# Head norm of the attention layers: token-major squares and Newton steps on VectorE, four transposes in place of a product with ones

## The chip, the cores and the metric

The kernel runs on one core of a Trainium2 chip. The metric is the device time of one execution in microseconds, the median of several runs. The engines are TensorE (PE in the rows, its weight loads PEld), VectorE (DVE), ScalarE (ACT), GpSimd (POOL) and SyncE (SP), which issues the weight loads from memory.

## The reference, cut to what matters

The program is a stack of four layers and a fifth block over 512 tokens of width 1024. Layers 0 and 3 are differential attention with 8 heads. Each head makes two softmax maps over causal keys, subtracts one from the other with a learned factor, multiplies by the values (128 wide), and normalises the 128 outputs of each token by their root mean square.

```python
for blk in range(S // BLOCK):                       # 4 blocks of 128 tokens
    s = einsum('bmqd,bmkd->bmqk', q[:, :, qs:ke], k[:, :, :ke]) + bias   # -inf above the diagonal
    a = softmax(s).reshape(B, H, 2, BLOCK, ke)
    a = a[:, :, 0] - lam_full * a[:, :, 1]
    outs.append(einsum('bhqk,bhkv->bhqv', a, v[:, :, :ke]))
o = concatenate(outs, axis=2)
o = rms_norm(o, subln) * (1.0 - lam_init)           # o * rsqrt(mean(o*o over 128) + 1e-6) * subln
return o.reshape(B, S, DA_V) @ w_out
```

All other layers are untouched.

## The kernel before, in words

Activations lie feature-major: 128 features on the partitions, 512 tokens along the row, 8 such chunks (`h`, and its high and low parts in fp32r, `gh`, `gl`, `xh`, `xl`). Every projection is three matmuls per chunk: high times high, high times low, low times high. Weights come in slabs of 1024x256 (`raw`), three of them in a ring: SyncE loads one when the unit of work that used its slot is done, GpSimd makes the high part `whi` (line 419), VectorE the low part `wlo` (line 1596). A unit is 8 chunks; its result lies in two banks of `proj` until ScalarE or VectorE has read it.

An attention layer (`da_mixer`, once for each engine) is a software pipeline written out by hand over 32 blocks, k = 4*head + block of 128 queries. Each engine has its own loop over k, with its own order, and semaphores between them. Every engine works strictly in its order. In iteration k TensorE does scores(k) into banks 0 and 1 of `mix`, then filling work, then transposes(k-2) of the attention map into bank 2, then values(k-3) into bank 3. The filling is the projection of the next pairs of heads: `da_fill` gives 14 chunks in 5 iterations, used up at k = 25. Q, K and V of a pair of heads are evacuated by ScalarE (`evac`, lines 1122 to 1126) and the first scores and values of a pair wait for that. From k = 26 the output projection is put in as far as heads are ready (`out_chunks`, in the order of `TAIL`, 1 or 2 chunks in each iteration); its last chunks of heads 6 and 7 come behind the loop.

VectorE does mask(k) (line 1828: adds the bias, takes the row maximum, both maps; line 1833 negates the maxima), coef(k-1) (reciprocals of the sums, lines 1840 and 1842), combine(k-1) (line 1851) and, in nine iterations, a `wlo`. ScalarE does second(k-1) (line 1144), exps(k) (line 1134, with an accumulator read each), an evacuation in nine iterations, and at_copy(k-2) (line 1152), which takes the transposed map out of bank 2.

The head norm before is feature-major. The outputs of a head lie in bank 3 as 128 features x 512 tokens. After values(4h+3) ScalarE squares the whole bank (`post_sq`, line 1093), TensorE multiplies it by a 128x128 matrix of ones into bank 2 (line 647, iteration 4h+7, right after the scores), which sums over the partitions and spreads the sum, ScalarE takes exp(-0.5*ln(sum/128 + eps)) (`post_rs`, lines 1101 and 1103, each behind a load of its function table), VectorE multiplies (`post_on`, line 1813), ScalarE writes the high part `xh` with the gain (line 1157) and VectorE the low part `xl` (line 1857). values(4h+4) waits until `post_on` has read bank 3, and transposes(4h+5) until the logarithm has read bank 2.

Of the kernel before, what the change touches and what calls it, by code (L numbers as in the profile page):

```python
# [18 lines left out]
F32 = mybir.dt.float32  # L19
# [5 lines left out]
P = 128  # L25
# [168 lines left out]
def build(nc, stream, xin, pin, pos, vecs, relb, onehot, eye, swap, picks, decay, out):  # L194
    with ExitStack() as ctx:
# [66 lines left out]
        post_rs = a("post_rs", [P, S])  # L262
# [101 lines left out]
        for name in ("start_pe start_act start_dve relu_done half_done h_half h_gate sg_half s1_added sq_done s2_added stats var_done "  # L364
                     "std_done norm_ready spread ln_u ln_full low_even half_x half_r r_hi p_in p_hi p_lo h_new scores masked negmax expd coef second "
                     "attn transposed at_copied av o_sq o_ms o_std o_rstd o_norm z_done "
                     "hg_prod hg_sc hg_pick hg_far_copied hg_keys hg_std hg_rstd hg_normed hg_turned kdup kcopy rot_in rot_mm rot_done decay_in "
                     "rsc rmul rav r_turned r_centred bias_in0 bias_in1 sw_bias0 sw_bias1 hi_even "
                     "hg_av sw_scores sw_masked sw_negmax sw_expd sw_attn sw_transposed "
                     "sw_v_turned sw_v_copied sw_at_copied sw_av sw_out sw_hi sw_lo pos_in trig z_ret rvar rstdd tap tap2 gelu2 stored "  # L370
                     "r_act u_act b_done hl_done z_lru mixed final_out lamsum lamexp lamprod").split():
            M(name)
# [64 lines left out]
        def _(pe):  # L437
# [148 lines left out]
            def da_mixer(d, layer):  # L586
# [30 lines left out]
                def transposes(k):  # L617
                    it = 32 * d + k
                    qb = k % 4
                    pe.wait_ge(M("attn"), it + 1)  # L620
                    if it:
                        pe.wait_ge(M("at_copied"), it)
                    if k > 4 and k % 4 == 1:
                        pe.wait_ge(M("o_std"), post_base(layer) + k // 4)
                    for kb in range(qb + 1):
                        last = nc.tensor.transpose(mix[:, 2, kb * P:(kb + 1) * P], da_a[:, k % 2, kb * P:(kb + 1) * P], ident[:, :])
                    last.then_inc(M("transposed"), 1)

# [26 lines left out]
                for k in range(32 + 4):  # L655
# [6 lines left out]
                    if k >= 26:  # L662
                        out_chunks(layer, (k - 26) * 12 // 10, (k - 25) * 12 // 10)
# [341 lines left out]
        def _(act):  # L1005
# [83 lines left out]
            def head_square(n, av_sem, av_value, buf):  # L1089
                act.wait_ge(av_sem, av_value)  # L1090
                if n:
                    act.wait_ge(M("o_ms"), n)
                A(buf[:, :], mix[:, 3, :], ACT.Square).then_inc(*own.sig(M("o_sq")))

            def head_std(n, buf):
                act.wait_ge(M("o_ms"), n + 1)
                if n:
                    act.wait_ge(M("o_norm"), n)
                mine()

                A(buf[:, :], mix[:, 2, :], ACT.Ln, scale=1.0 / P, bias=small[:, 252:253]).then_inc(*own.sig(M("o_std")))
                mine()
                A(buf[:, :], buf[:, :], ACT.Exp, scale=-0.5).then_inc(*own.sig(M("o_rstd")))

            def da_mixer(d, layer):
# [47 lines left out]

                def head_hi(hd):
                    n = post_base(layer) + hd
                    act.wait_ge(M("o_norm"), n + 1)
                    A(xh[:, hd, :], post_on[:, :], ACT.Copy, scale=small[:, 10 + d:11 + d]).then_inc(*own.sig(xh_ready if hd % 2 else M("hi_even")))
# [6 lines left out]
                for k in range(32 + 5):  # L1164
                    if layer == 0 and k == 18:
                        act.dma_start(bias_sw, bass.AP(tensor=table.tensor, offset=640 + 383, ap=[[1280, 16], [-1, P], [1, 256]])).then_inc(biased_sw, 16)
                    if 1 <= k < 33:
                        second(k - 1)
# [7 lines left out]
                    if k >= 7 and k % 4 == 3:  # L1176
                        head_hi((k - 7) // 4)
                    if 2 <= k < 34:
                        at_copy(k - 2)
                    if 3 <= k < 35 and (k - 3) % 4 == 3:  # L1180
                        n = post_base(layer) + (k - 3) // 4
                        head_square(n, M("av"), 32 * d + k - 3 + 1, post_sq)
                        head_std(n, post_rs)
# [392 lines left out]
        def _(dve):  # L1576
# [232 lines left out]
            def head_norm(n, buf, on):  # L1809

                dve.wait_ge(M("o_rstd"), n + 1)
                mine()
                V.tensor_tensor(on[:, :], mix[:, 3, :], buf[:, :], ALU.mult).then_inc(*own.sig(M("o_norm")))

            def da_mixer(d, layer):
# [38 lines left out]
                def head_lo(hd):  # L1854
                    dve.wait_ge(xh_ready if hd % 2 else M("hi_even"),
                                4 * X_GEN[f"mix{layer}"] + hd // 2 + 1 if hd % 2 else {0: 0, 3: 8}[layer] + hd // 2 + 1)
                    V.scalar_tensor_tensor(xl[:, hd, :], post_on[:, :], small[:, 10 + d:11 + d], xh[:, hd, :].bitcast(F32), ALU.mult, ALU.subtract)\
                        .then_inc(*own.sig(xl_ready if hd % 2 else None))
# [480 lines left out]
def post_base(layer):  # L2339

    return {0: 0, 3: 8}[layer]

# [104 lines left out]
```

## Time and profile before

| | |
|---|---|
| median of 3 runs | 3751.49 us (3750.78 to 3753.13) |
| the profiled execution | 3749.09 us |
| its span | 3746.4 us |
| granted TensorE clock, mean | 0.983 |
| TensorE busy | 3590.2 us (96%) |
| VectorE busy | 1831.0 us (49%) |
| ScalarE busy | 941.6 us (25%) |
| GpSimd busy | 847.4 us (23%) |

The span is the time between the first and the last instruction of the profile; the 2.7 us around it belong to the execution. Busy time of TensorE is modelled with overlapping matmuls, so 96% doesn't mean that it works at its peak. The two attention layers with their tails lie at 52 to 258 us (layer 0) and 2125 to 2331 us (layer 3).

### The profile page before, as it was taken

The numbers are of one execution on the slowest core, as the hardware profiler recorded it, in microseconds if no ns is written. First come the engines' busy times: TensorE is split into PE (matmuls) and PEld (weight loads), VectorE is DVE, ScalarE is ACT, GpSimd is POOL, SyncE is SP. The second block draws the span as 40 slices with busy tenths as digits, with TensorE's granted clock in tenths as the row PEclk, the third lists the DMA queues.
The fourth block names the chain that finished last, engine by engine and source line by source line (L and its number), as shares of the span: only waits on it lengthen the run. The fifth ranks groups of instructions, "written<-read, shape, count | busy, mean of one in ns | idle before, by whom it ended". The sixth has DMA issues, their size and how long they took to land.

```text
span 3746.4 us, 44571 instructions
## 1 busy us (share of the span) xinstructions
PE 3590.2 (96%) x18694; PEld 3031.5 (81%) x18694; DVE 1831.0 (49%) x2281; ACT 941.6 (25%) x1662; POOL 847.4 (23%) x374
## 2 busy tenths in 40 slices
PE   8989999999899999889999998999989999999998
PEld 6778888889788887578888876888878887788887
DVE  4555335546453346563335555553464436554434
ACT  3552001312220013531113265210141214221102
POOL 2113222211132223012223211322221111222221
PEclk9999999999999999999999999999999999999999
DMA  5312222211122222112222321222222222222222
GB/s 186 102 57 90 102 91 96 84 68 68 51 79 101 90 90 104 57 51 101 91 100 79 107 84 64 82 101 90 90 79 79 79 90 79 101 79 101 92 100 79
DMA packets 57279, 329.58 MB, mean 88 GB/s; under 512 B 5579, under 2 KB 12235, under 8 KB 20348
## 3 DMA queue, kind: packets, MB, share of 16 engines
q1 hardware_dynamic: 44604, 303.79, 22.7%
q10 hardware_dynamic: 12480, 22.96, 1.8%
q8 instruction: 151, 2.47, 0.3%
q14 instruction: 44, 0.36, 0.0%
HBM read 323.96 MB, written 8.80 MB: 89 GB/s over the span
## 4 chain that ended last, share of the span: by engine, by line
PE 87%; DVE 7%; ACT 4%; issue 1%; DMA 1%; POOL 0%; ACTq 0%; DVEq 0%
PE proj L441 23%; PE proj L443 22%; PE proj L442 22%; PE proj L540 2%; PE proj L541 2%; PE proj L542 2%; DVE s L1702 2%; PE proj L474 2%; PE proj L475 1%; PE proj L476 1%; DVE wlo L1596 1%; PE mix L613 1%; PE mix L707 1%; PE mix L517 1%; PE mix L639 1%
## 5 line engine op out<-in xcount | busy, mean ns | idle before, releaser
L419 POOL TENSOR_SCALAR whi<-raw 128x2048 fp32r<-128x2048 f32 x286 | 745.2, 2606 | 2616.4 <-DMA raw<-in_stream 2616.2
L441 PE MATMUL proj<-gh,whi 128*128 128x512 f32 x1968 | 785.0, 399 | 14.5 <-DVE wlo L1602 10.6
L443 PE MATMUL proj<-gh,wlo 128*128 128x512 f32 x1968 | 769.4, 391 | 0.0
L442 PE MATMUL proj<-gl,whi 128*128 128x512 f32 x1968 | 768.9, 391 | 0.0
L1596 DVE TENSOR_TENSOR wlo<-raw,whi 128x2048 fp32r<-128x2048 f32 x286 | 700.8, 2451 | 93.8 <-POOL whi L419 82.3
L441 PE MATMUL proj<-xh,whi 128*128 128x512 f32 x1760 | 694.7, 395 | 20.9 <-DVE wlo L1596 11.8
L443 PE MATMUL proj<-xh,wlo 128*128 128x512 f32 x1760 | 688.4, 391 | 0.0
L442 PE MATMUL proj<-xl,whi 128*128 128x512 f32 x1760 | 687.9, 391 | 0.0
L441 PEld LDWEIGHTS proj<-gh,whi 128*128 128x128 f32 x1968 | 371.4, 189 | 109.5 <-issue 19.3
L443 PEld LDWEIGHTS proj<-gh,wlo 128*128 128x128 f32 x1968 | 371.0, 189 | 79.4
L442 PEld LDWEIGHTS proj<-gl,whi 128*128 128x128 f32 x1968 | 371.6, 189 | 76.9 <-issue 2.2
L441 PEld LDWEIGHTS proj<-xh,whi 128*128 128x128 f32 x1760 | 332.4, 189 | 99.6 <-DVE wlo L1596 12.7
L443 PEld LDWEIGHTS proj<-xh,wlo 128*128 128x128 f32 x1760 | 332.1, 189 | 70.3
L442 PEld LDWEIGHTS proj<-xl,whi 128*128 128x128 f32 x1760 | 332.5, 189 | 69.0 <-issue 1.4
L1335 ACT ACTIVATE rl<-proj 128x1024 f32<-128x1024 f32 x64 | 65.7, 1027 | 951.3 <-PE proj L443 929.6
L1687 DVE TENSOR_TENSOR h<-h,proj 128x1024 f32<-128x1024 f32 (+1 forms) x76 | 80.0, 1052 | 351.4 <-PE proj L443 329.6
L2073 DVE SCALAR_TENSOR_TENSOR hid<-proj,rl 128x1024 f32<-128x1024 f32 x64 | 78.3, 1224 | 334.8 <-ACT rl L1335 334.7
L540 PE MATMUL proj<-xh,whi 128*128 128x256 f32 x640 | 191.1, 299 | 23.4 <-DVE wlo L1596 13.8
L541 PE MATMUL proj<-xl,whi 128*128 128x256 f32 x640 | 187.3, 293 | 0.0
L542 PE MATMUL proj<-xh,wlo 128*128 128x256 f32 x640 | 187.0, 292 | 0.0
L474 PE MATMUL proj<-whi,gh 128*128 128x256 f32 x512 | 152.1, 297 | 0.0
L540 PEld LDWEIGHTS proj<-xh,whi 128*128 128x128 f32 x640 | 129.3, 202 | 27.6 <-DVE wlo L1596 16.5
(295 smaller groups left out, 4417.7 us busy)
## 6 DMA issues: line engine op xcount, KB each, us to landing
raw<-in_stream SPq DMA_DIRECT2D x286, 1024.0 KB, 4.8
da_b<-bias_da ACTq DMA_DIRECT2D x16, 512.0 KB, 3.3
bias_da<-bias_rows ACTq DMA_DIRECT2D x8, 512.0 KB, 8.0
h<-in_x ACTq DMA_DIRECT2D x4, 512.0 KB, 8.9
bias_sw<-bias_table ACTq DMA_DIRECT2D x1, 2048.0 KB, 9.8
pf<-in_p ACTq DMA_DIRECT2D x4, 512.0 KB, 5.6
sw_b<-bias_sw ACTq DMA_DIRECT2D x4, 512.0 KB, 3.9
out_features<-fin SPq DMA_DIRECT2D x8, 256.0 KB, 2.3
```

The source lines that it names most:

```text
L419: nc.gpsimd.tensor_scalar(whi[:, n % RING], raw[:, n % RING], 1.0, 0.0, ALU.mult, ALU.add).then_inc(hi_done, 1)
L441: nc.tensor.matmul(out, wh, ah, start=first, stop=False, skip_group_check=check)
L442: nc.tensor.matmul(out, wh, al, start=False, stop=False, skip_group_check=check)
L443: return nc.tensor.matmul(out, wl, ah, start=False, stop=last, skip_group_check=check)
L474: nc.tensor.matmul(o, ah, wh, start=k == 0 and st % per == 0, stop=False, skip_group_check=True)
L540: nc.tensor.matmul(o, wh, ah, start=k == 0 and (j if own_banks else hf) == 0, stop=False, skip_group_check=True)
L541: nc.tensor.matmul(o, wh, al, start=False, stop=False, skip_group_check=True)
L542: last = nc.tensor.matmul(o, wl, ah, start=False, stop=k == 7, skip_group_check=True)
L1596: V.tensor_tensor(wlo[:, n % RING], raw[:, n % RING], whi[:, n % RING].bitcast(F32), ALU.subtract).then_inc(*own.sig(split_done))
L1687: ins = V.tensor_tensor(o, o, y, ALU.add)
L1702: V.tensor_tensor(total[:, :, cols(hf)], first if j == 1 else total[:, :, cols(hf)], value, ALU.add).then_inc(*own.sig(sem_))
L2073: V.scalar_tensor_tensor(hid[:, :, :], banks(u), 0.0, rl[:, :, :], ALU.max, ALU.mult).then_inc(*own.sig(rel["dve"]))
```

## The change

values(k) swaps its operands, so that a head's outputs lie in bank 3 token-major: 128 tokens on the partitions, and the 128 features of block b in columns 128b to 128b+127. ScalarE squares each block alone as soon as it is there, with the sum over the row in an accumulator (`small[:, 216+b]`). VectorE's `normalise` takes the four sums per partition, makes mean + eps, and the inverse root by a first guess from integer arithmetic on the bits and three Newton steps, all on 128x4 elements, and multiplies bank 3 by it into `post_o`. TensorE transposes the four blocks of `post_o` into bank 2 (`turn_back`), ScalarE copies them out with the gain (`take`) and makes the high part, VectorE the low part. The order in the loops changes with it: `normalise(h)` stands ahead of mask(4h+7) on VectorE, `turn_back(h)` behind scores(4h+8) on TensorE, and the high and low parts come one iteration later than before.

```diff
 # TensorE
-                    if k > 4 and k % 4 == 1:
-                        pe.wait_ge(M("o_std"), post_base(layer) + k // 4)
+                    if k >= 6 and qb == 2:
+                        pe.wait_ge(M("o_taken"), 8 * d + k // 4)
...
                     pe.wait_ge(M("at_copied"), it + 1)
+                    if k:
+                        pe.wait_ge(M("o_sq"), it)
                     if qb == 0 and k:
-                        pe.wait_ge(M("o_norm"), post_base(layer) + k // 4)
+                        pe.wait_ge(M("o_norm"), 8 * d + k // 4)
...
-                        last = nc.tensor.matmul(mix[:, 3, qb * P:(qb + 1) * P], da_v[:, g % 2, kb, hh * P:(hh + 1) * P],
-                                                da_at[:, k % 2, kb * P:(kb + 1) * P], start=kb == 0, stop=kb == qb)
+                        last = nc.tensor.matmul(mix[:, 3, qb * P:(qb + 1) * P], da_at[:, k % 2, kb * P:(kb + 1) * P],
+                                                da_v[:, g % 2, kb, hh * P:(hh + 1) * P], start=kb == 0, stop=kb == qb)
...
-                def mean_square(k):
-                    n = post_base(layer) + k // 4
-                    pe.wait_ge(M("o_sq"), n + 1)
-                    pe.wait_ge(M("at_copied"), 32 * d + min(k + 2, 32))
-                    nc.tensor.matmul(mix[:, 2, :], ones[:, :], post_sq[:, :], start=True, stop=True).then_inc(M("o_ms"), 1)
+                def turn_back(hd):
+                    pe.wait_ge(M("o_norm"), 8 * d + hd + 1)
+                    pe.wait_ge(M("at_copied"), 32 * d + min(4 * hd + 6, 32))
+                    for t in range(4):
+                        last = nc.tensor.transpose(mix[:, 2, t * P:(t + 1) * P], post_o[:, t, :], ident[:, :])
+                    last.then_inc(M("o_turned"), 1)
...
-                    if k >= 7 and k % 4 == 3:
-                        mean_square(k - 4)
+                    if k >= 8 and k % 4 == 0:
+                        turn_back((k - 8) // 4)
 # ScalarE
+                def square(k):
...
+                    act.wait_ge(M("av"), it + 1)
...
+                    A(post_sq[:, c], mix[:, 3, c], ACT.Square, accum_out=small[:, 216 + qb:217 + qb]).then_inc(*own.sig(M("o_sq")))
+                def take(hd):
+                    act.wait_ge(M("o_turned"), 8 * d + hd + 1)
...
+                    A(post_on[:, :], mix[:, 2, :], ACT.Copy, scale=small[:, 10 + d:11 + d]).then_inc(*own.sig(M("o_taken")))
...
+                    if 4 <= k < 36:
+                        square(k - 4)
                     if 1 <= k < 33:
                         second(k - 1)
...
-                    if k >= 7 and k % 4 == 3:
-                        head_hi((k - 7) // 4)
+                    if k >= 8 and k % 4 == 0:
+                        take((k - 8) // 4)
                     if 2 <= k < 34:
                         at_copy(k - 2)
-                    if 3 <= k < 35 and (k - 3) % 4 == 3:
...
+                    if k >= 8 and k % 4 == 0:
+                        head_hi((k - 8) // 4)
 # VectorE
+            def inverse_root(v, y, t):
                 mine()
+                V.tensor_scalar(t.bitcast(I32), v.bitcast(I32), 1, None, ALU.logical_shift_right).then_inc(*own.sig())
+                mine()
+                V.tensor_scalar(y.bitcast(I32), t.bitcast(I32), -1.0, 1597463007.0, ALU.mult, ALU.add).then_inc(*own.sig())
+                for i in range(3):
+                    mine()
+                    V.tensor_tensor(t, y, y, ALU.mult).then_inc(*own.sig())
+                    mine()
+                    V.scalar_tensor_tensor(t, t, -0.5, v, ALU.mult, ALU.mult).then_inc(*own.sig())
+                    mine()
+                    V.scalar_tensor_tensor(y, t, 1.5, y, ALU.add, ALU.mult).then_inc(*own.sig())
...
+                def normalise(hd):
+                    v, y, t = small[:, 220:224], small[:, 224:228], small[:, 228:232]
+                    dve.wait_ge(M("o_sq"), 32 * d + 4 * hd + 4)
+                    if hd or d:
+                        dve.wait_ge(M("o_turned"), 8 * d + hd)
+                    V.tensor_scalar(v, small[:, 216:220], 1.0 / P, RMS_EPS, ALU.mult, ALU.add).then_inc(*own.sig())
+                    inverse_root(v, y, t)
+                    mine()
+                    V.tensor_tensor(post_o[:, :, :], mix[:, 3, :].rearrange("p (t c) -> p t c", t=4),
+                                    y.rearrange("p (t c) -> p t c", c=1).broadcast_to([P, 4, P]), ALU.mult).then_inc(*own.sig(M("o_norm")))
...
                 for k in range(32 + 4):
+                    if k >= 7 and k % 4 == 3:
+                        if k < 33:
+                            coef(k - 1)
+                        normalise((k - 7) // 4)
                     if k < 32:
                         mask(k)
                     if 1 <= k < 33:
-                        coef(k - 1)
-                    if k >= 7 and k % 4 == 3:
-                        head_norm(post_base(layer) + (k - 7) // 4, post_rs, post_on)
-                    if 1 <= k < 33:
+                        if k < 7 or k % 4 != 3:
+                            coef(k - 1)
                         combine(k - 1)
-                    if k >= 8 and k % 4 == 0:
-                        head_lo((k - 8) // 4)
+                    if k >= 9 and k % 4 == 1:
+                        head_lo((k - 9) // 4)
```

## Rows read from the trace of the kernel before

**Rows 1.** The page's chain of work that ended last, by engine.
```profile
PE 87%; DVE 7%; ACT 4%; issue 1%; DMA 1%; POOL 0%; ACTq 0%; DVEq 0%
```

**Rows 2.** Windows: stretch, length, each engine's busy us, granted clock, DMA share, GB/s.
```profile
209.00:258.00 49.00, 39.20 (x176) 28.14 (x175) 21.73 (x53) 30.40 (x58) 3.89 (x1) 0.93 0.05 15
251.00:253.00 2.00, 2.00 (x6) 1.53 (x5) 0.00 (x0) 0.00 (x0) 0.00 (x0) 0.50 0.00 0
```

**Rows 3.** Waits of TensorE: us in total, times, longest.
```profile
PE mix L639 <- DVE post_on L1813: 9.0, 6, 2.1
```

**Rows 4.** Timeline around head 1: start, length, engine, line, operation.
```profile
111.09 1.06 PE L639 MATMUL mix<-da_at,da_v 128*128 128x128 f32 x8
...
112.19 0.60 ACT L1093 ACTIVATE post_sq<-mix 128x512 f32<-128x512 f32 x1 [0.19 <-PE mix L639]
...
113.14 1.13 PE L647 MATMUL mix<-post_sq,ones 128*128 128x512 f32 x2
...
113.25 0.69 DVE L1828 CUSTOM_DVE_ANT_0 da_s<-mix,da_b 128x512 f32<-128x512 f32 x1 [2.10 <-PE mix L613]
...
114.60 0.17 DVE L1833 TENSOR_SCALAR small<-small 128x2 f32<-128x2 f32 x1
...
117.57 0.71 ACT L1134 ACTIVATE da_s<-da_s,small 128x512 f32<-128x512 f32 x1
...
118.89 0.19 ACT L1134 ACTIVATION_READ_ACCUMULATOR da_s<-da_s,small 128x1 f32 x1
...
119.59 0.36 ACT L1152 ACTIVATE da_at<-mix 128x256 f32<-128x256 f32 x1
```

**Rows 5.** Timeline of TensorE, scores around heads 1 and 2.
```profile
118.74 0.49 PE L613 MATMUL mix<-da_k,da_q 64*128 64x128 f32 x4
...
136.61 1.13 PE L613 MATMUL mix<-da_k,da_q 64*128 64x512 f32 x4
...
144.57 0.61 PE L613 MATMUL mix<-da_k,da_q 64*128 64x128 f32 x4 [1.77 <-ACT da_k L1124]
```

**Rows 6.** Groups by line and shape, 52 to 258 us: busy, mean ns, idle before.
```profile
L626 PE MATMUL mix<-ident,da_a 128*128 128x128 f32 x80 | 13.9, 272 | 0.5 <-ACT da_at L1152 0.5
...
L1833 DVE TENSOR_SCALAR small<-small 128x2 f32<-128x2 f32 x32 | 8.3, 259 | 1.1
```

**Rows 7.** Timeline of VectorE at the start of the program.
```profile
32.84 1.17 DVE L1666 SCALAR_TENSOR_TENSOR small<-small 128x8 f32<-128x8 f32 x6
```

**Rows 8.** Timeline where GpSimd works on a weight slab.
```profile
87.06 3.01 POOL L419 TENSOR_SCALAR whi<-raw 128x2048 fp32r<-128x2048 f32 x1 [12.27 <-DMA raw<-in_stream]
...
88.68 1.13 PE L613 MATMUL mix<-da_k,da_q 64*128 64x512 f32 x4
...
137.66 1.91 POOL L419 TENSOR_SCALAR whi<-raw 128x2048 fp32r<-128x2048 f32 x1 [13.17 <-DMA raw<-in_stream]
...
139.13 0.46 DVE L1833 TENSOR_SCALAR small<-small 128x2 f32<-128x2 f32 x1
...
209.38 3.89 POOL L419 TENSOR_SCALAR whi<-raw 128x2048 fp32r<-128x2048 f32 x1 [16.39 <-DMA raw<-in_stream]
```

**Rows 9.** Timeline of the tail, TensorE and one VectorE row.
```profile
208.95 1.13 PE L613 MATMUL mix<-da_k,da_q 64*128 64x512 f32 x4
...
209.22 2.28 DVE L1596 TENSOR_TENSOR wlo<-raw,whi 128x2048 fp32r<-128x2048 f32 x1
...
217.80 0.79 PE L441 MATMUL proj<-xh,whi 128*128 128x512 f32 x1
...
229.28 1.13 PE L613 MATMUL mix<-da_k,da_q 64*128 64x512 f32 x4
...
235.00 0.46 PE L639 MATMUL mix<-da_at,da_v 128*128 128x128 f32 x2 [1.94 <-DVE post_on L1813]
...
241.98 1.05 PE L639 MATMUL mix<-da_at,da_v 128*128 128x128 f32 x8
...
250.11 0.47 PE L441 MATMUL proj<-xh,whi 128*128 128x512 f32 x1 [2.49 <-DVE xl L1857]
```

More of the change, by code:

```diff
@@ L261, in build @@
         post_sq = a("post_sq", [P, S])
-        post_rs = a("post_rs", [P, S])
+        post_o = a("post_o", [P, 4, P])
         post_on = a("post_on", [P, S])
@@ L365, in build @@
                      "std_done norm_ready spread ln_u ln_full low_even half_x half_r r_hi p_in p_hi p_lo h_new scores masked negmax expd coef second "
-                     "attn transposed at_copied av o_sq o_ms o_std o_rstd o_norm z_done "
+                     "attn transposed at_copied av o_sq o_norm o_turned o_taken lo_even z_done "
                      "hg_prod hg_sc hg_pick hg_far_copied hg_keys hg_std hg_rstd hg_normed hg_turned kdup kcopy rot_in rot_mm rot_done decay_in "
@@ L654, in da_mixer @@
                     pe.wait_ge(M("lamexp"), 1)
-                for k in range(32 + 4):
+                for k in range(32 + 5):
                     if k < 32:
                         scores(k)
-                    if k >= 7 and k % 4 == 3:
-                        mean_square(k - 4)
+                    if k >= 8 and k % 4 == 0:
+                        turn_back((k - 8) // 4)
                     for c in range(da_fill(k - 1), da_fill(k)):
                         chunk(c // 24 + 1, c % 24)
-                    if k >= 26:
+                    if 26 <= k < 36:
                         out_chunks(layer, (k - 26) * 12 // 10, (k - 25) * 12 // 10)
@@ L1087, in rms_chunks @@
                     A(out_hi[:, k, cols(hf)], tln[:, k % 4, :], ACT.Copy, scale=col(name, k)).then_inc(*own.sig(sem_))
[L1089 to L1103, printed above, removed]
             def da_mixer(d, layer):
@@ L1152, in at_copy @@
                     A(da_at[:, k % 2, 0:(qb + 1) * P], mix[:, 2, 0:(qb + 1) * P], ACT.Copy).then_inc(*own.sig(M("at_copied")))
+                def square(k):
+                    it, qb = 32 * d + k, k % 4
+                    c = slice(qb * P, (qb + 1) * P)
+                    act.wait_ge(M("av"), it + 1)
+                    if qb == 0 and k:
+                        act.wait_ge(M("o_norm"), 8 * d + k // 4)
+                    A(post_sq[:, c], mix[:, 3, c], ACT.Square, accum_out=small[:, 216 + qb:217 + qb]).then_inc(*own.sig(M("o_sq")))
+                def take(hd):
+                    act.wait_ge(M("o_turned"), 8 * d + hd + 1)
+                    if hd:
+                        n = hd - 1
+                        act.wait_ge(*((xl_ready, 4 * X_GEN[f"mix{layer}"] + n // 2 + 1) if n % 2 else (M("lo_even"), 4 * d + n // 2 + 1)))
+                    A(post_on[:, :], mix[:, 2, :], ACT.Copy, scale=small[:, 10 + d:11 + d]).then_inc(*own.sig(M("o_taken")))
                 def head_hi(hd):
-                    n = post_base(layer) + hd
-                    act.wait_ge(M("o_norm"), n + 1)
-                    A(xh[:, hd, :], post_on[:, :], ACT.Copy, scale=small[:, 10 + d:11 + d]).then_inc(*own.sig(xh_ready if hd % 2 else M("hi_even")))
+                    mine()
+                    A(xh[:, hd, :], post_on[:, :], ACT.Copy).then_inc(*own.sig(xh_ready if hd % 2 else M("hi_even")))
                 evac(0, 0)
@@ L1856, in head_lo @@
                                 4 * X_GEN[f"mix{layer}"] + hd // 2 + 1 if hd % 2 else {0: 0, 3: 8}[layer] + hd // 2 + 1)
-                    V.scalar_tensor_tensor(xl[:, hd, :], post_on[:, :], small[:, 10 + d:11 + d], xh[:, hd, :].bitcast(F32), ALU.mult, ALU.subtract)\
-                        .then_inc(*own.sig(xl_ready if hd % 2 else None))
+                    V.tensor_tensor(xl[:, hd, :], post_on[:, :], xh[:, hd, :].bitcast(F32), ALU.subtract)\
+                        .then_inc(*own.sig(xl_ready if hd % 2 else M("lo_even")))
+                def normalise(hd):
[5 more added lines that the diff above has]
+                    inverse_root(v, y, t)
+                    mine()
+                    V.tensor_tensor(post_o[:, :, :], mix[:, 3, :].rearrange("p (t c) -> p t c", t=4),
+                                    y.rearrange("p (t c) -> p t c", c=1).broadcast_to([P, 4, P]), ALU.mult).then_inc(*own.sig(M("o_norm")))
                 for j in range(3):
@@ L2336 @@
 RET_GATED = (5, 7, 10, 11)
-def post_base(layer):
-    return {0: 0, 3: 8}[layer]
 _ORDER = ["stream", "x", "p", "positions", "vectors", "rel_bias", "onehot", "eye", "swap", "picks", "decay"]
```

6 lines of the change are left out of this document (removed).

## The prediction

> **What bounds the kernel now.** I read the page first: TensorE holds 87% of the chain that ended last [rows 1]. So an edit counts only where it gives TensorE less to do or moves a moment at which TensorE waits. Then came the stretches of the attention layers by windows, the waits whose waiter is TensorE, and the timeline around one head. Each attention layer (0 and 3; layer 3 repeats layer 0's pattern) has a body, blocks 0 to 25, in which projection work fills TensorE, and a tail of 49 us from block 26 to the output projection, where TensorE is busy for 39 us and the granted clock averages 0.93 [rows 2]. The head norm makes TensorE wait 9.0 us for `post_on` over both layers [rows 3], and 2.49 us per layer for the last `xl` [rows 9]; nearly all of it is tail.
>
> Write k = 4h+b for block b of head h, and T for the end of values(4h+3), 0.07 us after scores(4h+3) begins. Around head 1, T is 112.15. ScalarE squares at once and the product with ones follows, while VectorE masks block 11 straight away, at 113.25. The exponentials of block 11 began only at 117.57, behind ScalarE's two table loads, two functions and one scaled copy, and the copy of block 9 out of bank 2 ended at 119.95, T + 7.8 [rows 4]. TensorE had finished scores(12) at 119.23 [rows 5] and went on filling: nothing waited for that copy.
>
> **The change part by part, TensorE's work.** The product with ones, 1.1 us in two passes [rows 4], goes. Four transposes come: one takes 0.27 us, and matmuls overlap by 0.1 to 0.16; 80 of them were busy for 13.9 us, 0.17 each [rows 6], so four take 0.65 us. The swapped operands of values cost nothing: 128 columns go through 128x128 weights either way. TensorE has 0.45 us less to do per head, 7 us in all, if nothing waits.
>
> **VectorE's chain.** New are 12 dependent operations on 4 elements (one scaling, two on integers, nine Newton) and one broadcast product of 512. Six dependent 8-element operations took 1.17 us [rows 7], so 0.20 us each: 2.4 us. The product reads PSUM like a mask of 512, 0.69 us [rows 4]; with 0.06 for handing over, 3.15 us. A small operation is bounded by 0.17 us, the negation of two maxima with nothing behind it [rows 4], and 0.26 us, the mean of those negations, held ones among them [rows 6]: 2.0 to 3.1 us for twelve. I take 0.20, from a chain of the same shape. The Trainium skill (VectorE: DVE Perf Modes, the section on the TRN2 errata) gives an fp32 tensor_tensor of N elements (N+151)/0.96 ns, 161 ns for 4: a fixed cost per instruction, which speaks against many small ones. By it the twelve would take 1.9 us, and each waiting head 0.5 us less than I sum; the trace's pitch, which includes the hand-over, is used.
>
> What is queued behind: `normalise` now stands ahead of mask(4h+3), which before ran at once. The mask, two reductions and a negation, takes 1.55 us [rows 4]. Then on ScalarE come its exponentials, 1.50 us, and at_copy(4h+1), 0.36 us [rows 4]. The new transposes write bank 2, so TensorE waits in turn_back for precisely that copy (`at_copied` 4h+6), with all its filling work queued behind. The old product waited for a copy one block earlier.
>
> **ScalarE.** One square of 0.60 us becomes four of 128 columns with an accumulator read. Bounds are 0.36, the copy of 256 columns without a read, and 0.6, the whole square [rows 4]; I take 0.45. Three of the four lie in ScalarE's idle time. Ln, Exp and both loads go, most of the 4.8 us between the square's end and 117.57 [rows 4]; a copy `take` of 0.6 us comes ahead of transposes(4h+6), under 3 chunks of filling in the body. ScalarE wins time, but its exponentials now wait for VectorE. The bias loads that it issues behind them are two heads ahead, and SP's weight loads follow TensorE's units: neither becomes late.
>
> **Sum of a body head.** 0.48 (square) + 0.05 + 3.15 (normalise) + 0.05 + 1.55 (mask) + 0.05 + 1.50 (exponentials) + 0.36 (copy) + 0.05 = T + 7.25, and 0.65 of transposes: filling resumes at T + 7.9. Before, it resumed at the end of the next scores, T + 7.1 at head 1 (heads 0 and 3 alike), and T + 8.5 at head 2 (head 4 alike), where scores wait for an evacuation to `da_k` [rows 5]. That evacuation stands ahead of the copy and adds 0.9 there. Hence 3 x 0.8 + 2 x 0.3 = 3.0 us.
>
> VectorE is also held while GpSimd works on a weight slab: a negation that began during GpSimd's 137.66 to 139.57 took 0.46 us and ended with it [rows 8]. Of normalise, operations would begin in such a stretch at head 0 (T = 88.75, GpSimd to 90.07), 0.65 us, and at head 2 (T = 136.68, to 139.57), 1.8 us [rows 8]. A slab subtraction on VectorE itself adds 0.3 at head 3. Body: 3.0 + 2.75 = 5.7 us per layer; 2.45 less if small operands are not held.
>
> **Sum of the tail.** Head 5 (T = 209.02): there are no 3 chunks of filling left, and VectorE subtracts a slab until 211.50, behind which coef(26) and then `normalise` come: it begins at T + 3.0 instead of T + 0.55, and GpSimd's hold (to 213.27 [rows 8]) adds 1.1. So the transposes end at T + 7.9 + 2.45 + 1.1 = 220.45, and filling resumes there, against 217.80 before [rows 9]: +2.65. The half-clock stretch that lies over this filling now also covers transposes, values and scores: +0.8. Head 6: filling went on behind values(28), which had waited until 235.00, 5.65 after T = 229.35; now it goes on at T + 7.9: +2.25, of which I take 0.65 as given back by the later wait for `da_at`, which then has passed: +1.6. Head 7: no mask lies between; from T = 243.03 to the waiting output chunk it was 7.1 us and is now 0.5 (square) + 3.15 + 0.75 (transposes) + 0.65 (`take`) + 0.7 (`xh`) + 0.8 (`xl`) = 6.55: -0.5 [rows 9]. Tail: +4.5.
>
> Per layer 10.2, two layers 20.4 us. The profiled execution took 3749.09 us (span 3746.4), so 3769.5; the median of the runs is 2.4 above it: 3772 us.
>
> **The rivals.** *The chain is hidden (faster).* Place: the wait of turn_back. At head 1 it vanishes if the copy lands by the end of scores(12), at 118.2 once the product is gone: the chain must be 1.1 us shorter than 7.25, so normalise at most 2.1 us. From there a head gains 0.45, and if the tail's waits go too, all that the old norm costs TensorE is won: 7 + 9.0 + 5.0 = 21 us, 3730 us. For it: ScalarE is rid of its table work. Against it: even before, the copy landed 0.7 us after the scores.
>
> *Half hidden (no change).* With a pitch of 0.15 us and no hold by GpSimd, 0.6 us less at each of 7 heads and 3.55 us of hold less per layer leave 2.5 us, 5 in two layers: 3757 us.
>
> *The clock.* The tail has two stretches at half the clock, 1.2 GHz, one of them behind the wait of 2.49 us [rows 2, 9]. A mean of 0.93 over 49 us is 3.4 us of full-speed work lost, 1.7 each [rows 2]. After, head 2 waits some 2 us, heads 5 and 6 3 us or more. If heads 0, 2, 3, 4 and 6 each bring on one more such stretch, that is 8.5 us per layer, 17 in all: 3789 us. The Trainium skill (TensorE: Matmul & The Clock Gate, Part 4, PE-mode transpose) says that a transpose does not count as activity of the array for its clock. By this rule the four transposes would not help to keep the clock where the product of 1.1 us did, which is this rival. The 160 transposes of before lie among matmuls at full clock, so its trace neither bears the rule out nor denies it.
>
> **How the numbers follow.** The wait moves to turn_back as summed: 0.60, own range 3760 to 3783 (small operations of 0.17 to 0.26 us, holds or none, tail terms half or one and a half). Clock: 0.12. Half hidden: 0.16. Hidden: 0.12. A measurement of this kernel tells a change over about 0.2%, 7.5 us, from none: slower 0.72, same 0.16, faster 0.12. The range from 3750 to 3790 takes in the half-hidden case and most of the clock's.
>
> **What would show it.** In the profile after: no table load in these layers' blocks; TensorE's transposes of `post_o` waiting for ScalarE's `da_at` copy, 1 to 2 us in the body and 3 us or more in blocks 28 and 32; twelve small VectorE operations 0.20 us apart, and the masks of 4h+3 at T + 3.7 instead of T + 1.1; each tail 4 to 5 us longer. I am wrong if those transposes wait for nothing, if the small operations run in less than 0.15 us each, or if ScalarE, rid of its loads, brings the copy forward anyway.

## The result and the profile after

The changed kernel takes 3777.03 us (median of 4 runs, 3776.55 to 3781.24), the kernel before 3751.14 us (4 runs, 3747.91 to 3753.13) on the same chip. The medians differ by 25.9 us, where 20.4 were forecast. The ratio, estimated from the single runs, is 1.0076 with a 95% interval of 1.0064 to 1.0088, or 0.76% slower; the quotient of the two medians is 1.0069. The profiled execution of the changed kernel took 3781.24 us with a span of 3779.4. It is the longest of the four, 4.2 us above their median, and 32 us above the profiled execution of before: sums over its trace have to be held against these 32 us, not against the 25.9.

The chain of work that ended last, from the page, against [rows 1]. TensorE's share fell by 2 points and VectorE's rose by 2.
```profile
PE 85%; DVE 9%; ACT 3%; issue 1%; DMA 1%; POOL 0%; ACTq 0%; DVEq 0%
```
The waits of TensorE in these layers (us in total, times, longest), against [rows 3]:
```profile
PE mix L649 <- ACT da_at L1139: 16.5, 10, 3.0
...
PE mix L641 <- DVE post_o L1877: 12.4, 6, 4.4
PE mix L613 <- ACT da_k L1111: 12.3, 4, 3.6
...
PE proj L441 <- DVE xl L1866: 4.5, 2, 2.3
...
PE mix L649 <- DVE post_o L1877: 1.6, 2, 0.8
...
PE mix L613 <- DVE small L1837: 1.5, 3, 0.6
```
L649 is the transposes of `post_o`, L641 values, L613 scores. The kernel before had 9.0 us for `post_on` [rows 3], and these:
```profile
PE mix L613 <- ACT da_k L1124: 5.6, 4, 1.8
PE proj L441 <- DVE xl L1857: 5.0, 2, 2.5
PE mix L647 <- ACT post_sq L1093: 4.4, 4, 1.5
PE mix L626 <- ACT da_at L1152: 0.9, 2, 0.5
PE mix L613 <- DVE small L1828: 0.6, 1, 0.6
```
So 25.5 us of waits became 48.8, and the largest is the one that the prediction named.

Now the windows over both attention layers whole, from the first copy to `da_q` to the first squares behind the layer. Columns: stretch, length, busy us of TensorE, its weight loads, VectorE, ScalarE, GpSimd, granted clock, DMA share, GB/s. Before:
```profile
38.00:256.00 218.00, 204.97 (x1159) 162.88 (x1158) 105.89 (x284) 117.16 (x253) 26.25 (x11) 0.98 0.28 97
...
2104.00:2328.00 224.00, 211.53 (x1195) 168.66 (x1194) 107.80 (x284) 118.42 (x253) 29.09 (x12) 0.98 0.22 76
```
After, and five stretches of layer 0 behind waits:
```profile
39.00:273.00 234.00, 208.50 (x1164) 168.85 (x1163) 121.24 (x379) 96.79 (x284) 28.40 (x11) 0.92 0.26 90
...
2123.00:2362.00 239.00, 215.10 (x1210) 174.26 (x1209) 123.19 (x380) 98.36 (x285) 30.25 (x12) 0.94 0.20 71
...
143.00:149.00 6.00, 2.28 (x11) 1.90 (x12) 5.07 (x14) 2.95 (x8) 0.00 (x0) 0.75 0.27 90
201.00:206.00 5.00, 4.80 (x23) 4.58 (x24) 2.21 (x9) 2.73 (x10) 0.00 (x0) 0.50 0.11 42
226.00:234.00 8.00, 6.09 (x23) 4.84 (x22) 3.49 (x14) 4.61 (x15) 0.00 (x0) 0.50 0.00 1
250.00:254.00 4.00, 4.00 (x14) 3.31 (x14) 0.75 (x1) 1.41 (x2) 0.00 (x0) 0.50 0.01 4
266.00:270.00 4.00, 3.61 (x9) 2.86 (x10) 0.25 (x1) 0.00 (x0) 0.00 (x0) 0.50 0.00 0
```
The two layers grow by 16 and 15 us. The long stretch between them, whose instructions are the same, took 1848 us before and 1850 after. Idle time of TensorE (length less busy) grew from 13.0 to 25.5 us in layer 0 and from 12.5 to 23.9 in layer 3. Its busy time should have fallen by 3.6 us per layer, the prediction's 0.45 per head of lighter work; it rose by 3.5 and 3.6. That is 7.1 and 7.2 us of busy time that no added work explains, and the clock column says where to look: 0.98 became 0.92 and 0.94. In layer 0 there are stretches at 0.50, which is 1.2 GHz, behind TensorE's waits at heads 4, 5, 6 and 7, and a mean of 0.75 at head 2 (at heads 2 and 4 the wait is for `da_k`). Behind the waits of 1.46 and 1.20 us at heads 0 and 1 the clock stayed at 1.00. Layer 3 is not the same: at its head 4 TensorE waited 2.30 us and kept 1.00.
```profile
2293.48 0.49 PE L613 MATMUL mix<-da_k,da_q 64*128 64x128 f32 x4 [2.30 <-ACT da_k L1111]
...
2294.00:2299.00 5.00, 5.00 (x43) 5.00 (x44) 1.81 (x8) 2.07 (x6) 0.00 (x0) 1.00 0.01 3
```
The length of a wait alone doesn't tell whether the clock falls. The kernel before had the same wait of 2.49 us for `xl` at the end of both layers; behind it the clock was 0.50 in layer 0 [rows 2] and 1.00 in layer 3:
```profile
2323.00:2328.00 5.00, 3.89 (x17) 3.25 (x18) 1.60 (x2) 0.18 (x1) 0.00 (x0) 1.00 0.00 0
```

The timeline of VectorE at head 4 (start, length, engine, line, operation), with a row of GpSimd among them:
```profile
192.72 0.17 DVE L1874 TENSOR_SCALAR small<-small 128x4 f32<-128x4 f32 x1 [1.74 <-ACT post_sq L1147]
192.92 0.17 DVE L1813 TENSOR_SCALAR small<-small 128x4 int32<-128x4 int32 x1
...
193.33 0.16 DVE L1818 TENSOR_TENSOR small<-small 128x4 f32<-128x4 f32 x1
...
194.91 0.16 DVE L1822 SCALAR_TENSOR_TENSOR small<-small 128x4 f32<-128x4 f32 x1
195.11 0.69 DVE L1877 TENSOR_TENSOR post_o<-mix,small 128x512 f32<-128x512 f32 x1
195.94 0.69 DVE L1837 CUSTOM_DVE_ANT_0 da_s<-mix,da_b 128x512 f32<-128x512 f32 x1
...
196.75 1.91 POOL L419 TENSOR_SCALAR whi<-raw 128x2048 fp32r<-128x2048 f32 x1 [15.29 <-DMA raw<-in_stream]
...
197.29 1.39 DVE L1842 TENSOR_SCALAR small<-small 128x2 f32<-128x2 f32 x1
```
Twelve small operations start 0.20 us apart. The negation behind the masks takes 1.39 us instead of 0.17 and ends with GpSimd's slab. At head 4 of layer 3 it took 0.78 us.

TensorE's scores of the last block of heads 4 to 7, and two waits of the tail:
```profile
168.05 0.70 PE L613 MATMUL mix<-da_k,da_q 64*128 64x512 f32 x2
192.21 0.70 PE L613 MATMUL mix<-da_k,da_q 64*128 64x512 f32 x2
218.29 0.70 PE L613 MATMUL mix<-da_k,da_q 64*128 64x512 f32 x2
225.66 0.77 PE L641 MATMUL mix<-da_v,da_at 128*128 128x128 f32 x2 [4.44 <-DVE post_o L1877]
242.62 0.70 PE L613 MATMUL mix<-da_k,da_q 64*128 64x512 f32 x2
249.82 1.09 PE L649 MATMUL mix<-ident,post_o 128*128 128x128 f32 x4 [3.02 <-ACT da_at L1139]
```

### The profile page after: what moved, and what is told of

Same layout as the page of the kernel before. It is cut to its first block, busy times and chain, and to the rows that moved or that the text cites. A ratio compares the mean times of both kernels' runs of the same rounds, so it can differ in the third digit from the quotient of the medians.

```text
span 3779.4 us, 44941 instructions
## 1 busy us (share of the span) xinstructions
PE 3601.9 (95%) x18726; PEld 3047.7 (81%) x18726; DVE 1869.0 (49%) x2473; ACT 901.2 (24%) x1726; POOL 850.4 (23%) x374
## 3 DMA queue, kind: packets, MB, share of 16 engines
q8 instruction: 152, 2.49, 0.3%
## 4 chain that ended last, share of the span: by engine, by line
PE 85%; DVE 9%; ACT 3%; issue 1%; DMA 1%; POOL 0%; ACTq 0%; DVEq 0%
PE proj L441 22%; PE proj L443 22%; PE proj L442 22%; PE proj L540 2%; PE proj L541 2%; PE proj L542 2%; DVE s L1703 2%; DVE wlo L1597 2%; PE proj L474 1%; PE proj L475 1%; PE proj L476 1%; PE mix L710 1%; PE mix L517 1%; PE mix L613 1%; PE mix L641 1%
## 5 line engine op out<-in xcount | busy, mean ns | idle before, releaser
L441 PEld LDWEIGHTS proj<-xh,whi 128*128 128x128 f32 x1760 | 334.9, 190 | 99.7 <-DVE wlo L1597 11.4
L414 POOL TENSOR_TENSOR xl<-h,xh 128x512 fp32r<-128x512 f32 (+1 forms) x80 | 99.3, 1243 | 233.1 <-ACT h L1082 233.1
## 6 DMA issues: line engine op xcount, KB each, us to landing
bias_sw<-bias_table ACTq DMA_DIRECT2D x1, 2048.0 KB, 10.3
```

Of the source, the lines that this page charges most:

```text
L414: nc.gpsimd.tensor_tensor(xl[:, k:k + n, cols(hf)], h[:, k:k + n, cols(hf)], xh[:, k:k + n, cols(hf)].bitcast(F32), ALU.subtract)\
L441: nc.tensor.matmul(out, wh, ah, start=first, stop=False, skip_group_check=check)
```

## The experiments

Theory W: the loss is TensorE's waits, made by the chain of square, normalise, mask, exponentials and copy. Rival C: much of it is the clock, because work behind the waits runs at 1.2 GHz. Rival O: the order on VectorE is all of it. Rival X: the four squares and their waits are the cost, and VectorE's small operations lie beside the path. Rival V: leaving out ScalarE's table loads is what the change is good for, so that a root on ScalarE would be slower still. Each run's ratio is to the kernel before on the same chip, with its 95% interval; several chips were used, so that times of two runs are compared through these ratios.

**Order on VectorE.** The mask and the coefficients go ahead of normalise:
```diff
-if k >= 7 and k % 4 == 3: (coef(k-1) if k < 33); normalise((k-7)//4)
-if k < 32: mask(k)
-if 1 <= k < 33: (coef(k-1) unless done); combine(k-1)
+if k < 32: mask(k)
+if 1 <= k < 33: coef(k-1)
+if k >= 7 and k % 4 == 3: normalise((k-7)//4)
+if 1 <= k < 33: combine(k-1)
```


> VectorE does mask(4h+3) and coef(4h+2) ahead of normalise(h), as before; all else is the changed kernel (3777 us). Theory W (TensorE waits for the end of the chain square, normalise, mask, exponentials, copy): the copy lands early, but values(4h+4) now waits for a normalise that ends 1.9 us later, at T + 5.6, and the next scores and the transposes follow it: filling resumes at T + 7.1 + 0.8, about where it does now. 3770 to 3780 us, with the waits of the transposes for da_at gone and longer ones of values for post_o in their place. Rival X (the cost is not VectorE's order but the four squares and their waits): also about 3777, but with the same waits as now. Rival O (the order alone is the cost): back to within 5 us of 3751.

Measured: 3766.35 us, 1.0048 (1.0033 to 1.0063). The waits of L649 for `da_at` are gone and those for `da_k` too; values now waits for the normalised head:
```profile
PE mix L641 <- DVE post_o L1877: 28.6, 12, 5.1
```
The time is 4 us under the range of theory W, so the order was worth more than forecast: from 0.76% to 0.48% over before, about a third of the loss, comes back. The rest stays, with another last link in the chain, so the order is not all of it (rival O).

**Order on TensorE.** The four transposes stand behind all but the last filling chunk of their block, in the tail behind the output chunk:
```diff
-if k >= 8 and k % 4 == 0: turn_back((k-8)//4)
 for c in chunks:
+    if turns and c == chunks[-1]: turn_back((k-8)//4)
     chunk(...)
```


> TensorE does turn_back(h) ahead of the last filling chunk of its iteration, or behind the iteration's output chunk where there is no filling, instead of right behind the scores; VectorE and ScalarE keep their order. Theory W: in the body the wait of 1.2 to 1.5 us at heads 0, 1 and 3 is covered by 1 to 2 chunks of 1.4 us, heads 2 and 4 wait for da_k and win nothing there, the two heads of the tail win 1.3 us each: 6 to 7 us per layer, 3763 to 3766 us. Rival C (most of the cost is the halved clock): what remains of idle time at heads 2, 4, 5, 6 still halves it, less than 4 us won, 3773 or more. Rival X: no change, 3777.

Measured: 3767.89 us, 1.0054 (1.0037 to 1.0070). The wait for `da_at` fell from 16.5 to 3.3 us, but transposes(4h+6) now wait 6.4 us for `take`, and those for `post_o` (12.3) and `da_k` (12.4) stay. It is 2 us over theory W's range and well below the 3773 of rival C, which as stated here (less than 4 us won) missed. Both moves together:

> Both moves together: mask(4h+3) and coef(4h+2) ahead of normalise(h) on VectorE, and turn_back(h) ahead of the last filling chunk (behind the output chunk in the tail) on TensorE. Alone they gave 3766 and 3768. Theory W: in the body values(4h+4) then waits only for post_o, 0.1 to 0.9 us at T + 5.6, and nothing waits for da_at or a late da_k: 3752 to 3758 us. If the two gains only added up (11 + 9) it is 3757. Rival X (squares and their waits cost by themselves): the waits go and the time stays over 3762.

Measured: 3769.99 us, 1.0059 (1.0047 to 1.0072), a miss by 12 us and no better than either move alone. The gains don't add up: the mask's move had already removed the wait that the late transposes avoid. What I had put at 0.1 to 0.9 us a head, the wait of values for `post_o`, is 28.7 us in this run, as with the mask's move alone (28.6).

**Length of the chain.** One Newton step instead of three, and six instead of three (`range(3)` becomes `range(1)` or `range(6)`; the first computes a coarser root):

> One Newton step instead of three: six small VectorE operations per head less, the inverse root is less exact. Theory W: 1.2 us of chain less in front of a waiting TensorE at each of 16 heads: 19 us at most, 3758 to 3762 us, and a few us more if halved stretches of the clock vanish too. Rival X (VectorE's small operations are beside the path): 3777. Rival C: halved stretches hang on the waits, so a little less waiting removes some of them or none: between 3750 and 3777 in a step.

> Six Newton steps instead of three: nine small VectorE operations per head more. Theory W: 1.8 us more at each of 16 heads, 29 us: 3803 to 3808 us, symmetric to the run with one step (per operation the same 0.2 us x 16). Rival X: 3777. Rival C: the clock adds steps of several us on top: over 3810.

Measured: 3753.29 us (1.0012, 1.0002 to 1.0021) and 3819.09 us (1.0187, 1.0171 to 1.0202). Against the kernel before on the same chip (3748.94 us) that is +4.4 and +70.2 us, and three steps are +25.9: the 96 operations between one and three steps cost 0.22 us each, the 144 between three and six 0.31. An operation's pitch is 0.20 us. Both runs missed the ranges of theory W alone (3758 to 3762 and 3803 to 3808), on either side, and the longer chain came out over 3810 as rival C has it; neither run tells the clock's share from that of GpSimd's holds. With one step the time lies far from the 3777 of rival X: the small operations are on TensorE's path, and the longer the chain gets, the more each microsecond of it costs.

With both moves and two steps:

> As the run with both moves, and two Newton steps instead of three (relative error of the root some 5e-6). normalise ends 0.6 us sooner, when the body no longer waits for it: theory W says that only the tail (heads 5, 6, 7) and the rest of the body's waits win, 3 to 4 us per layer: 3745 to 3750 us, at or below the kernel before (3749).

Measured: 3761.31 us, 1.0033 (1.0021 to 1.0046). A miss by 11 us: values still waited 19.6 us for `post_o`.

**The root on ScalarE.** Mask first, and v^-1/2 by two activations of 128x4 in place of all twelve small operations:
```diff
+ A(small[:, 224:228], small[:, 216:220], Ln, scale=1/P, bias=eps)
+ A(small[:, 224:228], small[:, 224:228], Exp, scale=-0.5)
- V.tensor_scalar(v, sums, 1/P, eps, mult, add); inverse_root(v, y, t)
```


> Token-major and with the four transposes, but the inverse root is Ln and Exp of 128x4 elements on ScalarE with its two table loads, as before, instead of thirteen small VectorE operations; VectorE masks first and waits for the root only ahead of its product; turn_back stays right behind the scores. Theory W: T + 0.5 + 2.6 (loads) + 0.5 (functions) and the product end at T + 4.4, the exponentials of block 4h+3 follow the root on ScalarE and the copy lands at T + 6.3, when the scores are just done: no wait in the body, 3745 to 3755 us. Rival V (leaving ScalarE's table loads is what the change is good for): slower than the run with mask first, over 3766 us.

Measured: 3749.62 us, 1.0007 (0.9998 to 1.0016), equal to before. Its waits and its windows:
```profile
PE mix L641 <- DVE post_o L1882: 10.6, 6, 3.5
...
39.00:253.00 214.00, 199.03 (x1171) 160.68 (x1170) 106.41 (x284) 120.48 (x316) 28.60 (x11) 0.98 0.28 97
```
Squares by block, four transposes and the broadcast product are all still there, and the loss is gone: it was made by the twelve operations and by their place, not by the token-major form. With the mask first in both, the twelve operations are worth the step from 1.0048 to 1.0007. This refutes X and V: the squares cost nothing that can be measured, and the table loads on ScalarE, back again, don't make it slower. The layer took 4 us less than before in this execution, which the median doesn't show.

**The clock.** Products with a matrix of zeros, added to a projection bank, fill TensorE's waits (the sums don't change). 63 per layer first:
```diff
+ for _ in range(n):   # n: 4 at turn_back of heads 0, 1, 5; 10 at 6; 11 at scores 16, 24; 17 and 2 at values 24, 28
+     nc.tensor.matmul(proj[...256], zeros, ones broadcast, start=False, stop=False)
```


> The changed kernel, with matmuls of a zero matrix added onto the bank that is being accumulated just ahead of TensorE's waits (heads 0, 1, 2, 4, 5, 6 of both layers; 52 per layer of 256 columns, some 0.24 us each at full clock, together a little less than the waits). They change no result and lie where TensorE idles. Theory W alone (only the waits cost): 3777 to 3780, no gain. Rival C (a good part is the clock that the waits halve; layer 3 shows 31 us at half the clock against 7 before): the halved stretches of the blocks vanish, 5 to 8 us won per layer, 3761 to 3767 us.

Measured: 3778.61 us, 1.0081 (1.0068 to 1.0095). The kernel that ran has 63 such products per layer, not the 52 of the expectation. The waits shrank from 49 to 11 us, but one product took 0.46 us (57.6 us for 126), about twice what I had allowed for, and the filler ran past the end of the waits. At head 5:
```profile
219.50 7.50 PE L655 MATMUL proj<-ones,zeros 128*128 128x256 f32 x34
```
The time is the one forecast for the waits alone, but with filler of 28.8 us per layer in waits of 24 the test decides nothing. So about half of it, 30 per layer:

> The changed kernel with the same filler as the run before with zero matrices, but about half of it: 30 zero products per layer (2 ahead of the turning back of heads 0, 1 and 5, 5 ahead of that of head 6, 5 ahead of scores(16) and scores(24), 8 and 1 ahead of the first products with values of heads 6 and 7), each about 0.46 us as measured there, so about 14 us per layer that should all lie inside the waits of some 25. Nothing on the other engines changes. If the granted clock is a cause of its own (work done at 1.2 GHz costs about 7 us per layer beyond the waits), the stretches of .50 behind the waits of heads 5 and 6 go or shrink and the time falls by 7 to 15 us, to 3762 to 3770. If the waits alone explain the loss, the time stays at 3775 to 3779.

Measured: 3767.74 us, 1.0049 (1.0036 to 1.0062), in the range that the clock's part had given and outside that of the waits alone (its five runs took 3762 to 3773 us). Its windows, first the work behind head 5's wait, which comes 5.7 us earlier here and has 0.50 in the changed kernel's 226:234:
```profile
221.00:229.00 8.00, 6.71 (x37) 4.83 (x38) 4.10 (x19) 5.48 (x17) 0.00 (x0) 1.00 0.00 1
...
38.00:262.00 224.00, 212.03 (x1234) 170.50 (x1233) 121.97 (x380) 96.85 (x285) 29.85 (x11) 0.99 0.28 94
...
2118.00:2351.00 233.00, 220.84 (x1272) 177.78 (x1271) 124.32 (x381) 98.13 (x285) 32.72 (x12) 0.99 0.21 73
```
TensorE does 14.6 us more per layer (29.2 us for 60 products), and the layers are 10 and 6 us shorter than the changed kernel's. Busy time without the filler is 197.4 and 206.2 us, against 208.5 and 215.1. Nothing but TensorE's activity in its waits was changed. One side effect would be a rival: work that comes earlier can miss a hold by GpSimd. It is small. The negation at head 4 took 0.78 us instead of 1.39 in layer 0 and 0.73 instead of 0.78 in layer 3, where the negation of block 18 took 1.67 instead of 1.04. So the clock is shown as a cause of its own. The whole program gains less than the two layers: it is 18.0 us over the kernel before where the changed kernel is 25.9. In the profiles that difference lies elsewhere: the unchanged stretch between them took 1850 us in the changed kernel's profile and 1856 in this one.

**GpSimd's hold.** In the last block of each head the 2-column negation becomes two 1-column ones:
```diff
-V.tensor_scalar(small[:, 104+c:106+c], small[:, 100+c:102+c], -1.0, None, mult)
+V.tensor_scalar(small[:, 104+c:105+c], small[:, 100+c:101+c], -1.0, None, mult)
+V.tensor_scalar(small[:, 105+c:106+c], small[:, 101+c:102+c], -1.0, None, mult)
```


> The changed kernel, the negation of the two row maxima (a 2-column operation on VectorE) done as two 1-column operations in the last block of each head. If it is the GpSimd slab operation that holds 2-column operations on VectorE and not 1-column ones, the negation that took 1.39 us in layer 0 takes about 0.2 twice, the exponentials of that block begin 1 us earlier, da_k is evacuated 1 us earlier and TensorE's wait for it at head 4 falls from 3.6 to about 2.5: 1 to 2 us less in all, 3775 to 3776. If VectorE is held whatever the width, one of the two takes 1.4 us and the time is that of the changed kernel or up to 2 us more (16 operations at 0.2).

Measured: 3774.85 us, 1.0067 (1.0054 to 1.0079), not to be told from the changed kernel. The timeline shows the hold move on:
```profile
197.62 1.91 POOL L419 TENSOR_SCALAR whi<-raw 128x2048 fp32r<-128x2048 f32 x1 [15.26 <-DMA raw<-in_stream]
...
198.22 0.15 DVE L1843 TENSOR_SCALAR small<-small 128x1 f32<-128x1 f32 x1
198.29 0.14 DVE L1844 TENSOR_SCALAR small<-small 128x1 f32<-128x1 f32 x1
198.35 1.58 DVE L1864 SCALAR_TENSOR_TENSOR da_a<-da_s,small,da_t 128x384 f32<-128x384 f32 x1
```
The 1-column operations ran at full speed inside GpSimd's stretch; the combination behind them took 1.58 us, against 0.60 in the changed kernel.

**Towards a faster kernel.** The root on ScalarE with the late transposes in the body, and then 12 zero products per layer in its waits:

> The kernel with the mask ahead of the normalise step and the inverse root by two activations on ScalarE, and in the body the four transposes of each head behind all but the last filling chunk of the block instead of ahead of them (unchanged in the tail, where there are no filling chunks). If the waits for da_at and post_o ahead of the transposes (7 us in all) still cost that much, 3743 to 3748; if the later transposes only push the ones of block 4h+6 behind the copy of head h, as it did when the Newton steps were kept, 3748 to 3752.

Measured: 3748.34 us, 0.9994 (0.9985 to 1.0003).

> The kernel of the run before it (mask first, inverse root on ScalarE, late transposes) with 12 zero products per layer placed in TensorE's waits of the tail: 1 and 2 ahead of the turning back of heads 5 and 6, 6 and 3 ahead of the first products with values of heads 6 and 7 (waits of 0.7, 1.1, 3.5 and 1.6 us there, 0.46 us a product). If what is left of the clock's price is in the stretch behind the wait of 3.5 us (3.4 us at 1.2 GHz per layer, which do 1.7 us of work at full clock), it goes and the time falls by 2 to 5 us to 3743 to 3746, under the kernel before. If the waits alone count, it stays at 3748; if the filler runs over the waits, 3748 to 3752.

Measured: 3749.37 us, 0.9999 (0.9990 to 1.0008). A miss. The window from 212 to 218 us, first in the kernel without the filler, then with it:
```profile
212.00:218.00 6.00, 4.35 (x19) 3.56 (x20) 3.06 (x10) 4.61 (x14) 0.00 (x0) 0.72 0.00 0
```
```profile
212.00:218.00 6.00, 4.31 (x22) 2.66 (x21) 3.16 (x11) 5.32 (x16) 0.00 (x0) 1.00 0.00 0
```
The half-clock work went, and no time came of it. The trace shows why at this place: with the filler the next transposes of the attention map wait 0.74 us for `take`, where without it they didn't wait, so the slower work had only filled that wait. I read from it that the clock costs something only where TensorE's own work sets the end of a stretch. No version was measurably faster than the kernel before.

## Why the prediction was right, point by point

**Direction and mechanism: right.** The wait moved to turn_back, for the copy of `da_at`, as the sum of a body head says. At head 1 (T = 112.59) that copy landed at T + 7.3, and 7.2 was the sum; TensorE waited 1.20 us for it. (Where it writes scores(4h+3) and mask(4h+3), block 4h+7 is meant, as its example of head 1 and block 11 shows.) At head 4, T is 192.28: normalise begins at T + 0.44 (0.53 in the sum), its product ends at T + 3.5 and the mask starts at T + 3.7, as forecast. Moving the mask removed exactly this wait, and with it about a third of the loss.

**Signs.** Two of them didn't come as written. At block 28 the transposes waited 1.31 us, not 3 or more, because values(24), just ahead of them, had already waited 4.44 us for `post_o`; their end, T + 11.9, is near the sum's T + 11.45. And each tail grew by 7.8 and 9.0 us, not by 4 to 5.

**VectorE's chain: right.** Twelve operations at a pitch of 0.20 and a product of 0.69 us. By the formula of the Trainium skill (VectorE: DVE Perf Modes, the section on the TRN2 errata) an fp32 tensor_tensor of 4 elements takes, as an estimate, 161 ns; the row of L1818 has 0.16, so it holds for the duration, and the 0.03 to 0.04 between two dependent ones comes on top of it. The square of 128 columns took 0.28 and its read 0.19, which begins before the square ends: 0.36 from start to end where I had taken 0.45. That is why normalise begins 0.09 earlier than in the sum.

**Heads one by one, layer 0.** The start of the last scores of a head, after less before, is a running delay. Rows of before that [rows 8, 9] don't have:
```profile
112.08 0.70 PE L613 MATMUL mix<-da_k,da_q 64*128 64x512 f32 x2
...
164.03 0.70 PE L613 MATMUL mix<-da_k,da_q 64*128 64x512 f32 x2
187.05 0.70 PE L613 MATMUL mix<-da_k,da_q 64*128 64x512 f32 x2
```
and of after:
```profile
88.13 0.70 PE L613 MATMUL mix<-da_k,da_q 64*128 64x512 f32 x2
112.52 0.70 PE L613 MATMUL mix<-da_k,da_q 64*128 64x512 f32 x2
137.84 0.70 PE L613 MATMUL mix<-da_k,da_q 64*128 64x512 f32 x2
```
The delay is -0.55, +0.44, +1.23, +4.02, +5.16, +9.34 and +13.34 us at blocks 7, 11, ... 31, and +17.2 at the layer's end. Its steps, with those of layer 3 and of the run with 30 zero products per layer, read from the same rows of their traces:

| Step, us | forecast | layer 0 | layer 3 | layer 0, filler | layer 3, filler |
|---|---|---|---|---|---|
| head 0 | 1.45 | 1.0 | 1.0 | 1.0 | 1.0 |
| head 1 | 0.8 | 0.8 | 0.5 | 0.8 | 0.8 |
| head 2, with the hold | 2.1 | 2.8 | 2.6 | 0.4 | 0.3 |
| head 3 | 1.1 | 1.1 | 1.3 | 1.2 | 1.9 |
| head 4 | 0.3 | 4.2 | 0.8 | 0.8 | 0.7 |
| head 5 | 3.45 | 4.0 | 3.7 | 2.0 | 2.0 |
| heads 6 and 7 | 1.1 | 3.8 | 5.3 | 0.4 | 2.0 |
| sum | 10.3 | 17.7 | 15.0 | 6.6 | 8.7 |

Where the filler keeps the clock up, the steps of heads 2, 5, 6 and 7 fall in both layers, and that of head 4 in layer 0; those of heads 0, 1 and 3 don't. The filler also takes away the half-clock work that the kernel before had, not only in layer 0's tail but at head 2 too (a granted clock of 0.60 from 144 to 148 us, which the prediction doesn't mention); so its columns lie under the forecast.

**Mis-sized: head 4 of layer 0.** I had looked for operations of normalise that begin inside a slab of GpSimd as the kernel before placed it. After the delays of heads 0 to 3 it was the negation of block 23 that met one (1.39 us). Behind it came the exponentials, then the copy to `da_k` at 200.14; scores waited 2.92 us, and the work behind them ran at half the clock. The hold is 1.2 us of the 3.9 us too many; with the filler 0.6 us of hold remained and the step was 0.8, so most of the rest is the clock's. In layer 3 the hold was shorter, the clock stayed up and the step was 0.8. That layer 3 repeats layer 0, as the prediction says, isn't so here. Splitting the negation alone freed nothing that can be measured, since the next operation was held.

**Mis-sized: the clock.** I had given the tail 0.8 us for it in the sum and left the rest to a rival at 0.12, priced at 8.5 us per layer. The mechanism was not a rival to the wait but came with it. By the windows it costs 7.1 us per layer more than before, at heads 2 and 4 to 7 in layer 0 and at heads 2 and 5 to 7 in layer 3. What is left of the layers' growth of 16 and 15 us, added idle time less the lighter work, is 8.9 and 7.8 us; the forecast without its clock term was 9.4. So the waits were slightly over-priced, and the clock nearly left out. By the profiles the two layers grew by 31 us where 20.4 were forecast; that the medians differ by only 25.9 brings the number nearer than the sum deserves. Six Newton steps are in line with it: 0.31 us for an operation of 0.20. Whether the four transposes count as activity, the rule beside that rival, no run here separates.

**Rivals.** "The chain is hidden" needed normalise at 2.1 us. With one Newton step it is 1.2 us shorter than the sum's 3.15, so the condition is met. Yet at head 1 TensorE still waited 0.42 us for the copy, and over all heads:
```profile
PE mix L649 <- ACT da_at L1139: 9.9, 9, 2.9
```
The time came to 0.12% over before. The old time was reached only with the mask first and the root on ScalarE; the 3730 never. Half hidden fell with the pitch of 0.20 and the hold, both measured.

## What to carry to other kernels

Before a computation moves to another engine, write down what is queued behind its new place and who waits for that; here the same work costs 26 us ahead of the mask, 17 behind it, and nothing measurable with the root by two activations on ScalarE. A chain of tiny dependent operations is priced by their number (0.20 us each, for 4 elements as for 8 here), not by their elements. Where a change gives TensorE new waits, price the work behind them at the lower clock too, if TensorE is what the next step waits for; here it stood behind waits of 2.26 to 4.44 us, but one of 2.30 in layer 3 kept the full clock.

## What the hardware showed unexpectedly

- VectorE operations on 2 or 4 columns stretch from 0.17 to 1.39 us (a negation) and 1.35 us (the first step of normalise at head 5) beside a GpSimd slab, while the 512-column mask that read PSUM in the same stretch kept its 0.69 us, and 1-column operations took 0.15. Not every operation of 2 columns is held: a reciprocal of 128x2 inside the slab of head 5 (at 220.94) kept 0.17.
- A product of zeros with 256 f32 columns costs 0.46 us of TensorE, in two passes. With such products in the wait at head 5, the granted clock behind it was 1.00 where it had been 0.50.
- 30 of them per layer, 14.6 us of useless work, made a layer 6 to 10 us shorter.
- The same wait of 2.49 us, at the end of both layers of the kernel before, had the clock at 0.50 behind it once and at 1.00 once.
